# Norms 2 and 3: scaling of tiles 1, 3, 5 moved to GpSimd, last three tiles' transposes placed in the next unit

## The reference

```
h = rms_norm(x, g_mix);  proj = h @ w_in
x = x + concat(gated_deltanet(...), indexed_sparse_attention(...)) @ w_out
h = rms_norm(x, g_xattn)                      # norm 2
x = x + memory_cross_attention(h, rms_norm(mem, g_mem), ...)
h = rms_norm(x, g_ffn)                        # norm 3
gate, up = split(h @ w_gu);  x = x + (silu(gate) * up) @ w_down
rms_norm(x, g) = x * rsqrt(mean(x * x) + 1e-6) * g
```

## Time and profile before

| | |
|---|---|
| median of 3 runs | 2014.24 us (2014.17 to 2015.78) |
| the profiled execution | 2009.58 us, of it the span of the trace 2007.9 us |
| mean granted TensorE clock | 0.952 |
| TensorE | busy 1875.3 us, 93% |
| VectorE, GpSimd, ScalarE | busy 1062.0, 685.7, 506.3 us |

### The profile page before, as it was taken

How to read it: one execution, slowest core, us unless ns; L and a number is a source line. 1 busy time by engine, 2 the same in 40 slices (tenths; PEclk the granted TensorE clock), 3 DMA queues, 4 the chain that set the end, 5 groups by cost and what they waited for, 6 DMA issues and landing times.

```text
span 2007.9 us, 27987 instructions
## 1 busy us (share of the span) xinstructions
PE 1875.3 (93%) x11001; PEld 1515.4 (75%) x11001; DVE 1062.0 (53%) x1750; ACT 506.3 (25%) x1010; POOL 685.7 (34%) x432
## 2 busy tenths in 40 slices
PE   6999999999978888889998969899999999999999
PEld 5888788777767777456786746688888888888887
DVE  4288889998966668666646034532232213232233
ACT  5366531122012222356404241301000100001000
POOL 4312233333333331056342301243433344434341
PEclk9999999999988888789998979899999999999999
DMA  7311011222210003000221100111111111111112
GB/s 228 84 32 32 22 43 53 63 92 87 94 65 1 2 2 126 12 1 2 85 74 42 43 0 21 32 38 56 45 49 50 44 52 48 46 42 52 52 42 84
DMA packets 111996, 102.36 MB, mean 51 GB/s; under 512 B 5099, under 2 KB 99358, under 8 KB 111646
## 3 DMA queue, kind: packets, MB, share of 16 engines
q1 hardware_dynamic: 109598, 92.68, 15.1%
q10 hardware_dynamic: 2304, 8.39, 1.0%
HBM read 87.42 MB, written 13.63 MB: 50 GB/s over the span
## 4 chain that ended last, share of the span: by engine, by line
PE 80%; DVE 14%; issue 3%; ACT 2%; POOL 1%; DMA 1%; DVEq 0%; ACTq 0%
PE ps L1213 8%; PE ps L1214 8%; PE ps L1215 8%; PE ps L399 6%; PE ps L401 6%; PE ps L400 6%; PE ps L371 5%; PE ps L372 5%; PE ps L373 5%; PE ps L877 3%; DVE top L1604 3%; DVE cacc L1619 2%; PE ps L972 2%; DVE score L1608 2%; PE ps L1083 2%
## 5 line engine op out<-in xcount | busy, mean ns | idle before, releaser
L682 POOL TENSOR_TENSOR WS<-WR,zero 128x1024 fp32r<-128x1024 f32 (+1 forms) x119 | 228.0, 1916 | 1009.9 <-PE ps L373 386.8
L684 POOL TENSOR_TENSOR WS<-WR,WS 128x1024 fp32r<-128x1024 f32 (+1 forms) x119 | 295.0, 2479 | 9.4
L1213 PE MATMUL ps<-HS,WS 128*128 128x512 f32 x704 | 274.7, 390 | 1.7 <-DVE HS L324 1.7
L1214 PE MATMUL ps<-HS,WS 128*128 128x512 f32 x704 | 274.5, 390 | 0.0
L1215 PE MATMUL ps<-HS,WS 128*128 128x512 f32 x704 | 274.3, 390 | 0.0
L371 PE MATMUL ps<-HS,WS 128*128 128x512 f32 (+1 forms) x656 | 261.0, 398 | 8.7 <-ACT raw L1314 3.9
L418 DVE TENSOR_TENSOR X<-X,ps 128x512 f32<-128x512 f32 x272 | 184.5, 687 | 156.1 <-PE ps L401 156.1
L372 PE MATMUL ps<-HS,WS 128*128 128x512 f32 (+1 forms) x656 | 257.5, 392 | 0.0
L373 PE MATMUL ps<-HS,WS 128*128 128x512 f32 (+1 forms) x656 | 257.4, 392 | 0.0
L1892 DVE TENSOR_TENSOR prod<-sil,ps 128x512 f32<-128x512 f32 x44 | 30.3, 688 | 402.2 <-PE ps L1215 402.2
L1608 DVE MATCH_REPLACE8 score<-top,score 128x1024 f32<-128x1024 f32 (+2 forms) x192 | 166.5, 874 | 0.0
(11 more groups left out here) (271 smaller groups left out, 2856.9 us busy)
## 6 DMA issues: line engine op xcount, KB each, us to landing
WR<-in_w_gu SPq DMA_DIRECT2D x44, 512.0 KB, 3.8
WR<-in_w_in SPq DMA_DIRECT2D x36, 512.0 KB, 3.8
WR<-in_w_down SPq DMA_DIRECT2D x22, 512.0 KB, 3.6
X<-in_x SPq DMA_DIRECT2D x8, 1024.0 KB, 8.3
dsa_spill<-cacc ACTq DMA_DIRECT2D x12, 512.0 KB, 2.6
KW<-in_w_xkv SPq DMA_DIRECT2D x8, 512.0 KB, 5.1
WR<-in_w_out SPq DMA_DIRECT2D x8, 512.0 KB, 3.7
out<-X SPq DMA_DIRECT2D x8, 512.0 KB, 2.6
```

What stands on the lines that cost most here:

```text
L682: pool.tensor_tensor(hi, w, bc(zero1[:, 0:1], [P, cols]), ALU.add).then_inc(w_hi, 1)
L684: pool.tensor_tensor(lo, w, hi.bitcast(F32), ALU.subtract).then_inc(w_split, 1)
L1213: pe.matmul(ps[:, b0 + half, :], lo, HS[:, 0, k, c], start=(k == 0), stop=False)
L1214: pe.matmul(ps[:, b0 + half, :], hi, HS[:, 1, k, c], start=False, stop=False)
```

## The change

For norms 2 and 3 alone (`last = TT - 2`; norm 1 keeps its way but for a wait of VectorE for its own scaling before):

- Tiles 1, 3 and 5 are scaled on GpSimd in two instructions: X times `gB` into `xn`, then, when `rs` is there, `xn` times `rs`. They stand in GpSimd's queue behind the split of unit `N_KV` (norm 2) and of the feed-forward unit j = 0 (norm 3), ahead of the next two splits. VectorE still takes their reciprocals.
- TensorE waits behind tile 4 for the remainders of tiles 0 to 4 only, starts the first half of the next up unit, and transposes tiles 5, 6 and 7 behind its second, fourth and sixth block of three products. The wait for all remainders stands ahead of the second half.
- The banks are arranged so that this works: tiles 0 to 5 in banks 0 to 3, tile 4 in the pair in which the next unit starts, tiles 6 and 7 in banks 4 to 7.
- The first round of the feed-forward loop is written out on TensorE and GpSimd; ScalarE's and VectorE's starting increments for the loop stand ahead of norm 3 instead of behind it.

```diff
             def bank(self, t, j):
-                return 2 * (t % self.nb) + j
+                return 2 * ((t + self.flip) % 2) + j + (4 if t >= self.last else 0)
...
+        def norm_pool_tile(pool, m, t, g_count):
+
+            if t == 1:
+                pool.wait_ge(gB_in, 16 * g_count)
+            m.ready(pool, t)
+            if t >= 2:
+                pool.wait_ge(m.tr, 2 * (t - 1))
+            link("p", pool, p_chain, pool.tensor_tensor(xn[:, t % 2, :], m.X[:, t, :], gB[:, :], ALU.mult))
+            pool.wait_ge(m.rs, t + 1)
+            pool.wait_ge(m.xn, t)
+            pool.tensor_tensor(xn[:, t % 2, :], xn[:, t % 2, :], bc(rs[:, t:t + 1], [P, D]), ALU.mult).then_inc(m.xn, 1)
+
         def norm_dve_tile(dve, m, t, g_count):
 
-            if t == 0:
-                dve.wait_ge(gB_in, 16 * g_count)
             dve.wait_ge(m.sd, t + 1)
             dve.reciprocal(rs[:, t:t + 1], sd[:, t:t + 1]).then_inc(m.rs, 1)
...
+            if m.last == m.n or t not in POOL_TILES:
+                if t == 0:
+                    dve.wait_ge(gB_in, 16 * g_count)
+                dve.wait_ge(m.rs, t + 1)
+                if t >= 2:
+                    dve.wait_ge(m.tr, 2 * (t - 1))
+                if t:
+                    dve.wait_ge(m.xn, t)
+                dve.scalar_tensor_tensor(xn[:, t % 2, :], m.X[:, t, :], rs[:, t:t + 1], gB[:, :],
+                                         ALU.mult, ALU.mult).then_inc(m.xn, 1)
...
         def norm_pe_tile(pe, m, t):
             pe.wait_ge(m.xn, t + 1)
-            if t >= m.nb:
-                pe.wait_ge(m.lo, 2 * (t + 1 - m.nb))
+            if 2 <= t < m.last:
+                pe.wait_ge(m.lo, 2 * (t - 1))
...
             for half, (c, w) in enumerate(chunks(width)):
+                if half and second:
+                    second()
...
             for n in range(N_OUT + RING, N_FF):
                 split_of(n)
+                if n == N_KV:
+                    for t in POOL_TILES:
+                        norm_pool_tile(pool, norm2, t, 2)
...
+                    if first and j == 0:
+                        for t in POOL_TILES:
+                            norm_pool_tile(pool, norm3, t, 3)
+
+            ff_round(0, first=True)
+            with pool.Fori(1, FFG) as g:
+                ff_round(g)
...
                         norm_pe_tile(pe, m, t)
+                    if r == 3:
+                        pe.wait_ge(m.lo, 10)
                 return after
 
-            def norm_after(m):
-                for t in range(5, TT):
-                    norm_pe_tile(pe, m, t)
-                pe.wait_ge(m.lo, 2 * TT)
+            def norm_between(m):
+
+                def between(i):
+                    if i in (1, 3, 5):
+                        norm_pe_tile(pe, m, (i + 9) // 2)
+                return between
+
+            def norm_rest(m):
+                return lambda: pe.wait_ge(m.lo, 2 * TT)
...
+                    up_pe(pe, N_KV, HS, SEQ, between=norm_between(norm2), second=norm_rest(norm2))
...
+                            if beside and half == 0:
+                                beside(k)
                         mm.then_inc(f_half, 1)
```

More of the change, by code:

```diff
@@ L283, in link, with __init__ @@
             eng.wait_ge(chain, linked[key])
+        POOL_TILES = (1, 3, 5)
         class Norm:
-            def __init__(self, tag, X, n, dst, ready, nb=4):
-                self.X, self.n, self.dst, self.ready, self.nb = X, n, dst, ready, nb
+            def __init__(self, tag, X, n, dst, ready, flip=0, last=None):
+                self.X, self.n, self.dst, self.ready, self.flip = X, n, dst, ready, flip
+                self.last = n if last is None else last
                 self.ss, self.sd, self.rs, self.xn, self.tr, self.hi, self.lo = (
@@ L358, in norm_pe, with up_pe @@
                 norm_pe_tile(pe, m, t)
-        def up_pe(pe, n, src, width, ncol=P, between=None):
+        def up_pe(pe, n, src, width, ncol=P, between=None, second=None):
             m = ups[n]
@@ L436, in build_layer @@
         cols_sb = sem("cols_sb")
-        norm1 = Norm("n1", X, TT, HS, lambda e, t: e.wait_ge(x_in[t // 2], 16), 2)
+        norm1 = Norm("n1", X, TT, HS, lambda e, t: e.wait_ge(x_in[t // 2], 16))
         nm_ss, nm_sd, nm_rs, nm_xn, nm_tr, nm_ev = (sem("nm_" + x) for x in ("ss", "sd", "rs", "xn", "tr", "ev"))
@@ L443, in build_layer @@
         m_in = sem("mem_in")
-        norm2 = Norm("n2", X, TT, HS, lambda e, t: e.wait_ge(down_add, 16 * 3 + 2 * t + 2), 2)
-        norm3 = Norm("n3", X, TT, HS, lambda e, t: e.wait_ge(down_add, 16 * 5 + 2 * t + 2), 2)
+        norm2 = Norm("n2", X, TT, HS, lambda e, t: e.wait_ge(down_add, 16 * 3 + 2 * t + 2),
+                     flip=ups[N_KV] % 2, last=TT - 2)
+        norm3 = Norm("n3", X, TT, HS, lambda e, t: e.wait_ge(down_add, 16 * 5 + 2 * t + 2), last=TT - 2)
         LV = range(1, 6)
@@ L782, in _, with ff_round @@
                 split_of(n)
-            land0 = [have[i] for i in range(RING)]
-            with pool.Fori(0, FFG) as g:
+                if n == N_KV:
+                    for t in POOL_TILES:
+                        norm_pool_tile(pool, norm2, t, 2)
+            def ff_round(g, first=False):
                 for j in range(PER):
@@ L1140, in _ @@
                         lambda s, half: pe.wait_ge(hs_lo, 2 * p + s + 1), norm_beside(norm2) if p == 3 else None)
-            norm_after(norm2)
             def xq_sums(u):
@@ L1150, in _ @@
             for u in range(4):
-                up_pe(pe, N_KV + u, HS, SEQ)
                 if u:
+                    up_pe(pe, N_KV + u, HS, SEQ)
                     xq_sums(u - 1)
+                else:
+                    up_pe(pe, N_KV, HS, SEQ, between=norm_between(norm2), second=norm_rest(norm2))
             pe.wait_ge(up_freed, ups[N_XO - 1] + 1)
@@ L1199, in _, with ff_round @@
                         lambda s, half: None, norm_beside(norm3) if p else None)
-            norm_after(norm3)
-            with pe.Fori(0, FFG) as g:
+            def ff_round(g, first=False):
                 for j in range(4):
                     slot, b0 = (N_FF + j) % RING, 2 * (j % 2)
+                    beside, rest = (norm_between(norm3), norm_rest(norm3)) if first and j == 0 else (None, None)
                     pe.wait_ge(w_split, g * PER + (N_FF + j + 1))
@@ L1210, in _ @@
                         c = slice(half * BANK, (half + 1) * BANK)
+                        if half and rest:
+                            rest()
                         for k in range(KT):
@@ L1219, in _ @@
                         lambda s, half: pe.wait_ge(f_lo, g * 4 + (2 * s + half + 2)))
+            ff_round(0, first=True)
+            with pe.Fori(1, FFG) as g:
+                ff_round(g)
         @block.scalar
@@ L1514, in _ @@
                                        ACT.Copy).then_inc(xohi, 1)
-            norm_act(act, norm3)
             for s in (f_sil, f_hi):
                 act.sem_inc(s, 1)
+            norm_act(act, norm3)
             with act.Fori(0, FFG) as g:
@@ L1878, in _ @@
                                           ALU.subtract).then_inc(xolo, 1)
+            for s in (f_prod, f_lo):
+                dve.sem_inc(s, 1)
             for p in range(2):
@@ L1881, in _ @@
             norm_after(norm3, 3)
-            for s in (f_prod, f_lo):
-                dve.sem_inc(s, 1)
             with dve.Fori(0, FFG) as g:
```

## The result

| | before | changed |
|---|---|---|
| median | 2013.57 us (6 runs, 2011.21 to 2015.78) | 1990.46 us (6 runs, 1988.62 to 1998.29) |
| ratio, 95% interval | | 0.9891 [0.9873, 0.9909] |
| the same kernel in a later comparison | 2012.16 us (9 runs) | 1992.10 us (5 runs), 0.9905 [0.9889, 0.9922] |
| span of the trace | 2007.9 us | 1986.9 us |
| mean granted TensorE clock | 0.952 | 0.961 |

The change makes the kernel 1.0 to 1.1% faster, 19 to 22 us by the two ratios.

The account below looks back on a forecast made before the run. TensorE, 80% of the chain, bounds the kernel, so only its waits or low clock around norms 2 and 3 give time. Gains 7.2 + 7.4 = 14.6 us gave 1995.0, plus 4.7 for the median: 1999.6 us, range 1995.3 to 2007.5.

Parts of the forecast that it names:

- The schedule: Norms 2 and 3: tiles 1 and 3 hidden, first half from 1077.5, held splits free; gains 7.2 and 7.4 us.
- the signs named beforehand: Profile after: 5.2 us to the first product, second half some 12 us behind the first, tile 7's scaling near 2.5.
- I take 1.2 GHz, 0.427 us a product: TensorE from 1077.5 in norm 2: low clock after the wait, six products 2.56 us and not 1.36.
- Rival (c): Clock still high at 1077.5, tile 7's scaling slips ahead of the split: gains 9.1 and 9.4, 1995.7 us; chance 0.13.
- I take the same difference off it: Whole kernel: the median lies 4.7 us above the profiled execution, turning 1995.0 into the forecast 1999.6 us.
- The exclusion: VectorE scalings and GpSimd splits exclude each other; tile 7's scaling waits, by shared bandwidth done some 1.3 us earlier.
- Rival (a): Clock stays low through the first half because transposes lie between its products: gain 3.2 in all, 2011 us; chance 0.12.
- (b): Clock falls again while TensorE waits 1 to 2 us for tile 7: one norm 2003.5, both 2007 us; chance 0.20.
- (d): GpSimd's pair of products costs more than 4.4 us; at 13 each norm loses 6: 2026 us; chance 0.03.
- (e): Interleaving does nothing: second half also at 1.2 GHz, 1.7 us later than before a norm: 2018 us; chance 0.02.

Follow-up runs that it names:

- experiment 2: Against the kernel before: tiles 1, 3, 5 scaled on GpSimd and the loop's first round written out, but no interleaving; 2008.26 us, ratio 0.999.
- Experiment 5: The changed kernel with GpSimd's next two weight splits held until tile 7 is scaled; 1991.65 us, ratio 0.9908 to the kernel before.
- experiment 7: The changed kernel with splits held, tile 7's root early and the first half started behind tile 3; 1987.51 us, ratio 0.988 to the kernel before.
- experiments 1 and 3: Changed kernel with all tiles scaled on VectorE (1: 2003.46 us), or with TensorE also waiting behind tile 4 for tile 6's scaled data (3: 2002.75 us).
- experiment 10: The kernel before plus needless products: two behind tile 3, four behind tile 4, one each behind 5, 6, 7; 2004.72 us, single run.
- experiment 4: The changed kernel, start held for tile 6's scaled data, with twelve needless products in the wait; 2001.75 us, ratio 0.9963 to the kernel before.
- experiment 9: The changed kernel, start held for tile 6's scaled data, with seven needless products in the wait; 2000.48 us, single run.
- experiment 8: The kernel before plus needless products behind tiles 4 (five), 5 (two), 6 and 7 (three each); 2012.17 us, ratio 0.9999.

## Why the prediction missed

**The schedule was right.** Tile 3 and tile 4 hidden, the first half 5.2 us behind the pair's end (5.06), GpSimd's products at 2.4 and 1.9 (2.37 and 1.90), no cost from the held splits, the moved gain row or the written-out round: TensorE waits for no split, and the feed-forward stage is the same to 0.1 us. Of the signs named beforehand, the second half came 9.78 us behind the first and not 12, and tile 7's scaling took 2.04 and not 2.5; the first follows from the next point.

**The step that failed is "I take 1.2 GHz, 0.427 us a product"**, with the clock at 1.00 in all ten norms of the changed kernel. It rested on the transposes of the earlier trace rows at 1.97 us, tile 5's. But the clock had fallen before the wait of 3.74 ahead of them, 3.6 us behind the pair's end, in the middle of tile 4's transposes:

```profile
1075.38 1.52 PE L352 MATMUL ps<-ident,xn 128*128 128x128 f32 x8 [2.02 <-DVE xn L336]
```

and the clock from 1076.00 up to the first product:

```profile
1076.00:1089.79 13.79, 6.81 (x29) 0.50 0.34 106
```

In norm 3 it fell at 4.0. There 1.03 us of transposes, an empty 2.02 and more transposes had gone before; in the changed kernel tiles 3 and 4 follow each other (2.06) and one wait of 3.00 follows. That wait is longer than 2.02, so a shorter wait is not what kept the clock. The runs show that it held in 14 of 16 norms, or 16 of 18 with experiment 2; why it holds behind the one order and falls behind the other stays open. From the step came the late arrival of tile 5, and from that the late scaling of tile 7: 17.3 us to the second half instead of 14.84. Experiment 5 shows the price in one profile, 2.5 us for one norm, and 2.5 twice is the 5 us by which 14.6 falls short of 19.5. That is the price with the splits held; no run of the changed kernel itself has a fallen clock, so for it the 2.5 is an inference. Rival (c), the clock high at 1077.5, had the mechanism, and its 15.4 us to the second half and 18.5 us of gain come within 0.5 and 1.0 of what was measured. I had given it 0.13.

**The rest of the distance.** With the clock right the forecast would have been 2014.24 less 19.5, 1994.7: still 4.2 us above the median measured, and just below the range. The second term mis-sized is "I take the same difference off it": the median before was 4.7 us above its profiled execution, the median after only 1.8 above its own (1990.46 against 1988.62). That is 2.8 us, and with the 1.5 us by which the stretches without a change differ it makes up the 4.2. I can't put either down to the change: the kernel before had medians from 2009.63 to 2013.57 in the comparisons of this study. By the later comparison's ratio, 0.9905, the gain is 19.1 us, close to the 19.5 of the stretches.

**The exclusion** of scalings and splits was right as a mechanism. Its sum was 0.5 us a norm too long: I put the end of the two-operand split 11.5 us behind the pair's end, it was 11.0 (1082.4). The splits started when I had them start (5.8 behind against 5.9); but the two-operand one took 3.26, 0.9 more than the next one beside no scaling (1085.31, 2.40), where I had added a whole scaling of 1.28. The exclusion costs 1.0 us a norm (experiment 5, norm 2, 13.86 against 14.84), where the prediction had some 1.3. The Trainium skill's rule that the two exclude each other (SBUF — State Buffer, section Who interferes with whom) agrees with the trace: tile 7's scaling took 2.04 while a split ran and 1.28 with the splits held (experiment 7).

**Rival (a)**, the clock low for the whole first half because transposes lie in it, is excluded where it could be seen: in norm 3 of experiment 5 the half began at 1.2 GHz, and the clock was back at 1267.0, behind nine products and eight transposes. In both norms of experiments 1 and 3 it came back 4.2 to 5.3 us into the half as well, with transposes in between. Whether transposes alone would bring it up, which the Trainium skill denies (TensorE: Matmul & The Clock Gate, section Part 4: PE-mode transpose), no run here shows. (b), a fall in the wait for tile 7, did not occur in any profile of the changed kernel, with that wait at 0.85 us. (d) and (e) fell with the durations of GpSimd's products and the clock column.

**Where the 19.5 us come from.** The clock is worth 2.7 of the 9.65 us a norm in the kernel before (experiment 10). The remaining 7, by subtraction, are overlap: the half starts 12.4 us sooner and carries three tiles' transposes. The sum of the parts (10.7) is so far below the whole because each uses the other. Against interleaving alone the changed kernel gains 5.4 us in norm 2 (14.84 against 20.25): its half starts 4.5 us sooner, at 5.06 and not at 9.52, and takes 0.9 less, at the higher clock (9.78 against 10.73). GpSimd alone has the data as early and no half to start with it. Both parts alone also lose the clock, from 3.5 and 3.9 us behind the pair's end on with interleaving alone, from 7.0 and 7.3 on with GpSimd alone; how the difference splits between clock and overlap no run shows.

## What to carry to other kernels

When a change alters what TensorE does and waits for in a stretch, price the stretch at both clock levels and give the high one weight: the row of the old kernel shows the clock behind the old order of work and waits, not behind the new one. Look up where in the old stretch the clock fell, too. Two changes that each give little can be worth double together, if one makes data early and the other lets TensorE use it. Measure such a change in the profile, between two instructions that every version has: there it repeated within 0.02 us, while the medians of one kernel moved by 2 and more.

## What the runs showed of the hardware

- TensorE's clock held through 2.06 us of transposes and 3.00 us empty in 14 of 16 cases; where 1.03 of transposes, 2.0 empty and one more tile's transposes came first, it fell 3.6 and 4.0 us behind the pair's end in the kernel before (granted clock 0.60 and 0.61 in the earlier trace rows). The length of a wait alone does not tell.
- A needless float32 product of the identity with 512 columns took 0.81 to 0.86 us at a clock of 1.00 (twelve in 9.74 us in experiment 4, seven in 6.01 in experiment 9), where the split products of 128 x 512 follow each other in 0.23.
- Filling TensorE's waits with needless products made the kernel before faster, though it does more: 2.7 us a norm in experiment 10. Thirteen of them instead of nine, overrunning by 1.6 us, took it all back in experiment 8.
